# A three-stage transformer and state-space block on one core: GpSimd forms the low parts of three of every 18 weight chunks of the head groups

## The reference, cut to what matters

```python
u = rms_norm_2(h, norm_mix[i])
proj = u @ w_in[i]                                   # 1024 x 11808
y_a = conformer_conv_branch(proj[..., OFF_CONV:OFF_Z], ...)      # 31 taps on 1024 channels
y_b = ssd_branch(proj[..., OFF_Z:OFF_XBC], proj[..., OFF_XBC:OFF_DT], ...)   # 4 groups of 8 heads
y_c = swa_branch(...)
# in conformer_conv_branch
h = a * jax.nn.sigmoid(gate)
h = causal_depthwise_conv(h, dw_w, dw_b)
h = layer_norm(h, ln_g, ln_b)
# in ssd_chunked, per group of heads
scores = cb[:, :, :, None] * decay
y_diag = jnp.einsum("bcgrqs,bcsgrp->bcqgrp", scores, xdt)
```

## Time and profile before

| | |
|---|---|
| median of three executions | 1461.05 us (1457.92, 1461.05, 1463.77) |
| the profiled execution | 1458.56 us |
| its span | 1456.7 us |
| mean granted TensorE clock, share of full speed | 0.988 |
| TensorE matmul, busy | 1380.3 us, 95% |
| VectorE, busy | 1033.2 us, 71% |
| ScalarE, busy | 893.6 us, 61% |
| GpSimd, busy | 329.0 us, 23% |
| DMA, mean rate over the span | 161 GB/s |

### The profile page before, as it was taken

The page is one execution under the profiler, slowest core; times in us unless marked ns, Lnnn a source line. Parts: engine busy times, 40 slices in busy tenths (PEclk is TensorE's granted clock), DMA queues, the critical chain, the costliest instruction groups (busy, mean ns, idle before and its releaser), DMA issues.

```text
span 1456.7 us, 29899 instructions
## 1 busy us (share of the span) xinstructions
PE 1380.3 (95%) x11462; PEld 1266.4 (87%) x11462; DVE 1033.2 (71%) x1567; ACT 893.6 (61%) x1694; POOL 329.0 (23%) x320
## 2 busy tenths in 40 slices
PE   6998999998998999999899998989899799999999
PEld 6888999997887999998788887978788699899998
DVE  6787855567577666569888999766896576566554
ACT  5455744467587555558778786767675455665443
POOL 2000411124002111125744435200500012331100
PEclk9999999999999999999999999999999899999999
DMA  8332555554932655544444443433555254355652
GB/s 321 124 117 87 177 200 200 183 195 146 200 122 99 229 192 201 191 157 157 162 145 149 142 145 120 146 120 112 174 171 174 87 174 150 111 182 195 202 186 75
DMA packets 35608, 233.80 MB, mean 161 GB/s; under 512 B 4000, under 2 KB 7072, under 8 KB 8352
## 3 DMA queue, kind: packets, MB, share of 16 engines
q1 hardware_dynamic: 31104, 223.75, 44.7%
q10 hardware_dynamic: 3216, 4.19, 1.9%
q0 software_dynamic: 1168, 4.20, 1.0%
HBM read 227.93 MB, written 4.19 MB: 159 GB/s over the span
## 4 chain that ended last, share of the span: by engine, by line
PE 49%; DVE 10%; ACT 4%; issue 3%; POOL 1%; DMA 0%; ACTq 0%; DVEq 0%; POOLq 0%
PE ps L464 7%; PE ps L465 7%; PE ps L474 7%; PE ps L533 4%; PE ps L534 4%; PE ps L539 4%; DVE w_lo L1902 3%; PE ps L872 2%; PE ps L873 2%; PE ps L876 2%; ACT w_hi L1190 2%; DVE arena L2317 1%; POOL arena L2703 1%; PE ps L516 1%; PE ps L920 1%
## 5 line engine op out<-in xcount | busy, mean ns | idle before, releaser
L1902 DVE TENSOR_TENSOR w_lo<-raw,w_hi 128x1024 bf16<-128x1024 f32 x420 | 539.8, 1287 | 253.5 <-ACT w_hi L1190 253.3
L1190 ACT CAST w_hi<-raw 128x1024 fp32r<-128x1024 f32 x420 | 438.5, 1047 | 339.0 <-PE ps L474 133.7
L464 PE MATMUL ps<-xa_both,w_hi 128*128 128x256 f32 x1296 | 324.7, 292 | 12.3 <-ACT w_hi L1190 10.7
L465 PE MATMUL ps<-xa_both,w_hi 128*128 128x256 f32 x1296 | 307.3, 279 | 0.0
L464 PEld LDWEIGHTS ps<-xa_both,w_hi 128*128 128x128 f32 x1296 | 245.8, 190 | 18.3 <-issue 12.3
L465 PEld LDWEIGHTS ps<-xa_both,w_hi 128*128 128x128 f32 x1296 | 246.1, 190 | 0.7 <-issue 0.2
L533 PE MATMUL ps<-xb_both,w_hi 128*128 128x256 f32 x832 | 204.7, 288 | 0.1
L534 PE MATMUL ps<-xb_both,w_hi 128*128 128x256 f32 x832 | 195.1, 277 | 0.0
L474 PE MATMUL ps<-xa_bf,w_lo 128*128 128x256 bf16 x1296 | 169.4, 274 | 2.0 <-DVE w_lo L1902 1.9
L872 PE MATMUL ps<-xb_both,w_hi 128*128 128x256 f32 x592 | 151.0, 296 | 7.8 <-DVE arena L2317 6.5
L533 PEld LDWEIGHTS ps<-xb_both,w_hi 128*128 128x128 f32 x832 | 156.6, 188 | 1.6 <-DVE xb_both L1917 0.3
(11 more groups left out here) (339 smaller groups left out, 2372.2 us busy)
## 6 DMA issues: line engine op xcount, KB each, us to landing
raw<-weights SPq DMA_DIRECT2D x210, 1024.0 KB, 4.9
band<-arena ACTq DMA_DIRECT2D x1, 3072.0 KB, 35.5
arena<-band POOLq DMA_DIRECT2D x8, 256.0 KB, 3.2
arena<-gla_masks SPq DMA_DIRECT2D x1, 1088.0 KB, 15.4
H<-x_t SPq DMA_DIRECT2D x2, 512.0 KB, 5.0
arena<-band POOLq DMA_DIRECT2D x8, 128.0 KB, 2.6
arena<-mem_t POOLq DMA_DIRECT2D x1, 1024.0 KB, 5.1
out_t<-H ACTq DMA_DIRECT2D x8, 128.0 KB, 2.0
```

The source lines that it names most:

```text
L464: mm(ps[:, bank, 0:T], w_hi[:, s, k], X.hi[:, k], start=k == 0, stop=False)
L465: mm(ps[:, bank, 0:T], w_hi[:, s, k], X.lo[:, k], start=False, stop=False)
L1190: nc.scalar.copy(w_hi[:, j % HI_SLOTS].rearrange("p k n -> p (k n)"), raw[:, j // 2 % RING, j % 2]).then_inc(hi_done, 1)
L1902: TT(w_lo[:, j % HI_SLOTS].rearrange("p k n -> p (k n)"), raw[:, j // 2 % RING, j % 2], w_hi[:, j % HI_SLOTS].rearrange("p k n -> p (k n)" ...
```

## The change

The low parts of the chunks that VectorE would cut in slots 1, 5 and 9 of groups 0 to 2 (the chunks of slots 4, 8 and 12, nine chunks in all) are cut by GpSimd, in front of the convolution addition whose products are the first made in that slot or after it. TensorE waits for these chunks on a semaphore of their own, `pool_lo`. So that `lo_done` still counts chunks in order, VectorE skips a count and, two chunks further, waits for GpSimd's part and adds 2.

```diff
@@ module level
+POOL_LO_AT = (1, 5, 9)
+CONV_PRODUCTS = 38
+POOL_LO = [R_LEAD + R_GROUP * g + i + 3 for g in range(3) for i in POOL_LO_AT]
@@ semaphores
+        pool_lo = sem("pool_lo")
@@ TensorE, region_chunk
-                pe.wait_ge(lo_done, c + 1)
+                if s in POOL_LO:
+                    pe.wait_ge(pool_lo, POOL_LO.index(s) + 1)
+                else:
+                    pe.wait_ge(lo_done, c if s - 1 in POOL_LO else c + 1)
@@ VectorE, cut_lo
-                if isinstance(c, int) and c >= CHUNKS:
+                if isinstance(c, int) and (c >= CHUNKS or c - C_R in POOL_LO):
                     return
                 dve.wait_ge(hi_done, c + 1)
+                after_pool = isinstance(c, int) and c - 2 - C_R in POOL_LO
+                if after_pool:
+                    dve.wait_ge(pool_lo, POOL_LO.index(c - 2 - C_R) + 1)
                 TT(w_lo[:, j % HI_SLOTS].rearrange("p k n -> p (k n)"), raw[:, j // 2 % RING, j % 2],
-                   w_hi[:, j % HI_SLOTS].rearrange("p k n -> p (k n)").bitcast(F32), ALU.subtract).then_inc(lo_done, 1)
+                   w_hi[:, j % HI_SLOTS].rearrange("p k n -> p (k n)").bitcast(F32),
+                   ALU.subtract).then_inc(lo_done, 2 if after_pool else 1)
@@ GpSimd
+            lo_at = [0]
+            def products_by(s):
+                n = CONV_PRODUCTS + 5 * (R_LEAD // 2)
+                for i in range(R_LEAD, s):
+                    n += PRODUCTS_AT[(i - R_LEAD) % R_GROUP]
+                return n
+            def low_part(s):
+                c = C_R + s
+                pool.wait_ge(hi_done, c + 1)
+                G.tensor_tensor(w_lo[:, c % HI_SLOTS].rearrange("p k n -> p (k n)"), raw[:, c // 2 % RING, c % 2],
+                                w_hi[:, c % HI_SLOTS].rearrange("p k n -> p (k n)").bitcast(F32), ALU.subtract).then_inc(pool_lo, 1)
             for pair in range(len(POOL_TAPS) // 2 // TAPS):
                 both = c_out[:, 2 * pair:2 * pair + 2]
                 for k in range(1, TAPS):
                     a = PAIR_ADDS * pair + k - 1
                     pool.wait_ge(ca["prod"], 2 * (TAPS * pair + k + 1))
+                    while lo_at[0] < len(POOL_LO) and products_by(POOL_LO[lo_at[0]] - AHEAD) < 2 * (TAPS * pair + k + 1):
+                        low_part(POOL_LO[lo_at[0]])
+                        lo_at[0] += 1
                     if k > 1:
                         pool.wait_ge(ca["add"], a)
```

## The result

The changed kernel takes 1475.49 us, the median of four runs (1474.27 to 1476.87), against 1459.49 us for the kernel before, timed again beside it (1457.44 to 1463.77). The ratio is 1.0106, with a 95% interval of 1.0079 to 1.0133. That is slower, as forecast, but by 16 us and not by 5, and it lies 0.5 us above the top of the range. The profiled execution took 1475.09 us (span 1473.0).

The account below looks back on a forecast made before the run. PE was taken to be bound, with 11.7 us of waits on VectorE's merge and scaling. Merge delays of 1.3 + 2.0 + 1.7 = 5.0 us gave 1463.6, or 1466 us on the median's scale; range 1455 to 1475.

Parts of the forecast that it names:

- What bounds it: In the groups, PE waits only for VectorE, on the merge (5.9 us) and the scaling of inputs (5.8 us).
- The low part's price: Each GpSimd subtraction of 128x1024 takes 2.5 us, with bounds of 2.4 to 2.6.
- Slot 1: The low part blocks VectorE's cut of slot 2; PE's transposes come 0, 1.2 and 0.8 us later in groups 0 to 2.
- Slots 5 and 9, the merge: Slot 5's gain is given back; slot 9's low part delays the merge, 1.3, 2.0 and 1.7 us by group, slot 1 included.
- One addition gets in: In group 1's merge, one queued GpSimd addition slips in behind slot 9's low part, costing 1.3 us.
- the sum itself: Merge delays in the three groups, counted as PE's delay: 1.3 + 2.0 + 1.7 = 5.0 us slower.
- The bound of +11.7 us: Upper bound: all nine low parts on the path for their length less the cut replaced, 9 x (2.5 - 1.2).
- rival C: ScalarE held up: products delayed 2.3 us in slots 6 and 10, casts reach PE late; 13 us, 1474 us; chance 0.15.
- A: Relief: VectorE reaches the merge 2.4 us earlier, PE's wait there shrinks by 5.0 us, giving 1456 us; chance 0.20.
- The point named for it: For relief to hold, a low part must block VectorE by less than 1.2 us on average.
- B: Nothing on PE's path: freed time and blocking both vanish in VectorE's waits for high parts; 1461 us; chance 0.20.
- C's two signs: In the profile after, PE waits for casts, or ScalarE waits for additions, by over 5 us.

Follow-up runs that it names:

- the fills: Changed kernel with each of GpSimd's nine low parts replaced by zero fills that read nothing from SBUF: 1456.69 us with one fill each, 1454.68 with three.
- the half-length run: Changed kernel with GpSimd's nine low parts covering 512 of 1024 columns, the other half left out: 1459.10 us, 0.9993 of the kernel before.
- three fills: Changed kernel with three zero fills of 0.95 us, one behind the other, in place of each low part: 1454.68 us, 0.9948 of the kernel before.

## Why the prediction was right in kind and short in size

**What bounds it.** Right: the waits that changed are the two that the prediction named, and no other wait of PE in the groups grew. The mechanism, a low part that shuts out VectorE's two-input instructions in front of what PE waits for, is the one that the fills confirm.

**The low part's price.** Taken at 2.5 us, measured 2.40; the estimate from the Trainium skill's GPSIMD Engine Reference was 2.25, so the rows were the nearer source by a little. The size decided nothing.

**Slot 1.** Right within a fifth of a microsecond: the wait on the scaling was to grow by 0, 1.2 and 0.8 us and grew by 0, 1.0 and 0.6, to 1.78, 3.2 and 2.41 us.

**Slots 5 and 9, the merge.** Mis-sized. Beyond the delay of slot 1 the walk gave 1.3, 0.8 and 0.9 us, 3.0 in all. The waits on the merge grew by 2.0, 1.2 and 1.7, 4.9 in all. "One addition gets in" was too few: in group 0 an addition got in behind the low part, between the two L2383 (2.4 and 1.3 us long), and another between the two L2389. And in groups 0 and 2 the low part of slot 5 didn't stand behind the product L2357 but in front of it: as L2368 it took 2.78 and 2.80 us. In group 2 the low part of slot 9 also came before the merge, into the four multiplies in front of it (L2396), which took 6.59 us.

**The term that was missing.** The step that failed is the sum itself. It priced waits of PE at their length, with the sentence that the merge's "delay is PE's". Half of the loss, 7.7 of 14.2 us, is matmuls at half clock behind those waits. The page of before had the clue that such a thing happens: its clock is 0.988 over the span though it is 1.00 in the groups, so the clock is lower somewhere else. A clock term belonged in the range's upper end. The bound of +11.7 us, every low part on the path, fell short for the same reason: the groups lost 14.2. The top of the range came from rival C, and the time came out there by another cause.

**The rivals.** A fell for the reason that was given, and the fills, which leave that work out, show what it would have been if GpSimd's work shut nothing out: 1454.68 us, against the 1456 it was put at. The point named for it (a hold under 1.2 us) agrees with the half-length run. B fell. One of C's two signs, ScalarE's wait for additions over 5 us, came true by a little: 5.6 us in the groups. But PE waits for no cast, and with three fills ScalarE waits 9.5 us in a kernel that is faster than before, so that wait doesn't make the loss, and the sign was drawn too near. (C's six delays of 2.3 us are 13.8 us and not 13.)

**What would show it.** Low parts of 2.4 to 2.6, some stretched (up to 3.0, not 3.7), cuts of up to 2.9 us (2.87) and VectorE's busy time kept were all there. The waits went to 18.2 us where some 16 were put; the prediction's own sum of 5.0 would have made 16.7.

## What to carry to other kernels

Before work goes from VectorE to GpSimd, look at what each reads: a GpSimd instruction that reads SBUF and a VectorE one with two SBUF inputs run one after the other, and here the copy on GpSimd is twice as long as what it replaces. Here a GpSimd instruction as long as the VectorE one it replaced broke even, one twice as long cost 1.1%, and a short one gained 0.4%; the share of busy time on GpSimd says nothing about that. (That the move would pay where VectorE has only one-input work beside it follows from the traces, but wasn't run.) And longer waits of PE have to be priced with the slow matmuls that can stand behind them, which doubled the loss here. No length separates the waits that have them from those that don't: in these traces waits of 1.87 to 5.01 us had them, and others of 2.24 and 3.28 us hadn't.

## What the runs showed that was not expected

The clock term: 3 us at half clock behind a wait of 3.35 us, which makes such a wait cost some 1.5 us more than it lasts (group 0: 2.0 us more of wait and 1.5 us more up to the next output sum, 5.08 in place of 3.56).

Three fills, 2.9 us together, beside VectorE's busiest slots cost nothing that can be measured: their ratio, 0.9948, is no worse than the 0.9960 with low parts of 0.2 us. In these traces a GpSimd that only writes leaves VectorE's two-input instructions at their normal length.

The slow stretches don't keep their place: two traces of one kernel, with the same waits on merge and scaling within 0.1 us, have theirs in different groups.

Additions already took time from the kernel before. Holding them back at three places, by a wait and no other change, is worth 0.26%.
